# Two transformer blocks in float32: how the experts are dealt to the two sides of the array, and in which order their weights are loaded

## The chip, the cores and the metric

One core of a Trainium2 chip runs the whole program. The metric is device microseconds of one execution.

## The reference

All data are float32. A first block (attention, a window attention, pooling, a long convolution, then a mixture of experts) is followed by a second block (a recurrence with attention, retention, two SwiGLU layers). The change lies in the mixture of experts of the first block, on 512 tokens of width 1024:

```python
N_EXPERTS, TOP_K, D_MODEL, D_EXPERT = 16, 2, 1024, 512
# each token picks one group of four experts, then the best two of that group
gates = jnp.sum(jax.nn.one_hot(eidx, N_EXPERTS) * w[..., None], axis=1)
for e in range(N_EXPERTS):
    h = jax.nn.silu(x @ w1[e]) * (x @ w3[e])
    out = out + gates[:, e:e + 1] * (h @ w2[e])
```

The inputs that the reference draws (seed 0) send this many of the 1,024 (token, expert) pairs to experts 0 to 15: 34, 40, 52, 30, 54, 16, 66, 66, 47, 127, 193, 87, 52, 44, 63, 53. In units of 64 tokens, rounded up, these are 1, 1, 1, 1, 1, 1, 2, 2, 1, 2, 4, 2, 1, 1, 1, 1, together 23.

## The kernel before, in words

TensorE (PE) multiplies, VectorE (DVE) and ScalarE (ACT) take its products, GpSimd (POOL) gathers and scatters token rows, and SP issues the loads of weights. All weights come as tiles of 512 KB into `weights_and_work`.

**A job.** The expert stage is a loop of `n_jobs` jobs on PE (`experts()`). One job works on two units at once: 64 tokens of an expert on side 0 of the array (b = 0) and 64 tokens of another on side 1 (b = 1). Each side has one buffer of 12 tiles (`expert_w[b]`) for its expert: tiles 0 to 3 and 4 to 7 hold w1 and w3, tiles 8 to 11 hold w2. I call these three groups of four tiles phases 0, 1 and 2. A job runs phases 0 and 1 (L1353, 64 matmuls), turns the token rows of the next job (L1337) and the hidden rows of this one (L1362), and runs phase 2 (L1371, 32 matmuls). Behind each tile it raises `e_passed`. At its head it reads one number, `landing`, into a register (L1344), and ahead of each tile it waits once, for that tile's semaphore `e_landed[s]` to reach it.

**The deal.** Even experts go to side 0 and odd ones to side 1, in order of their number, each for as many jobs as it has units. `n_jobs` is the larger of the two sums. `first` is the job with which an expert begins.

**The loads.** SP loads experts 0 and 1 ahead of the stage. The other 14 are loaded in order of `first`, in a loop with a turn for each expert (L804). A turn reads three numbers (L805 to L807), and for each of the 12 tiles a fourth (L809), waits until that tile of that buffer has been passed by the job before and until the semaphore's last load has landed, and issues the DMA (L812). So the second of two experts that begin with the same job is issued behind all 12 tiles of the first.

**The tables.** The numbers that SP and PE read are made by DVE on tiny tiles in `router()`: it ranks the tokens (`rank`), places them in jobs, and makes `gather_i`, then `landing_i`, `n_jobs_i` (`jobs_ready`), `result_i`, and last `order_i`, `after_i` and `buffer_i` (`order_set`). `link` makes DVE wait for its own last instruction. PE's `experts()` begins with a wait for `jobs_ready`, and POOL gathers the rows of the first job as soon as `gather_i` is set.

Of the kernel before, what the change touches and what calls it, by code (L numbers as in the profile page):

```python
# [6 lines left out]
ALU = mybir.AluOpType  # L7
ACT = mybir.ActivationFunctionType
AX_X = mybir.AxisListType.X
# [8 lines left out]
S = 512  # L18
# [41 lines left out]
EXPERT_TILES = 12  # L60
UNIT = 64
# [123 lines left out]
def plan():  # L185
# [62 lines left out]
    r["ms_meta"], = b.many(1)  # L248
# [122 lines left out]
def two_blocks(nc, d):  # L371
# [5 lines left out]
    with ExitStack() as ctx:  # L377
# [69 lines left out]
        buffer_of = tiny[:, 460:460 + EXPERTS]  # L447
# [81 lines left out]
        order_hot, order_t = piece(arena, 14000, EXPERTS, EXPERTS), piece(arena, 14260, EXPERTS, EXPERTS)  # L529
        order, first, landing_e = (arena[:, a:a + EXPERTS] for a in (15640, 15656, 15672))  # L530
        order_f = piece(arena, 15700, 3, EXPERTS)
        order_i, landed_i, buffer_i = (arena[:, 15760 + EXPERTS * i:15760 + EXPERTS * (i + 1)].bitcast(I32) for i in range(3))
        after_f = piece(arena, 15940, EXPERT_TILES, EXPERTS)
        after_i = piece(arena, 16140, EXPERT_TILES, EXPERTS).bitcast(I32)
        over = piece(arena, 17700, JOBS, EXPERTS)
        landing_f = arena[:, 15820:15820 + JOBS]
        landing_i = arena[:, 15880:15880 + JOBS].bitcast(I32)
# [96 lines left out]
        e_landed = [sem(f"expert_tile_in_{i}") for i in range(RING)]  # L634
        e_passed, order_set = sem("expert_tiles_passed"), sem("expert_order_set")
# [88 lines left out]
        def _(sp):  # L724
# [53 lines left out]
            def first_of(e, i):  # L778
                if e:
                    sp.wait_ge(e_landed[slots[i]], 16)  # L780
                elif i < RING - 4:
                    sem_, value = read_by(before + i - RING)
                    sp.wait_ge(sem_, value)
                else:
                    ready(sp, r["w_out"][2 * (i - RING + 4) + 1])
                sp.dma_start(expert_w[e][:, slots[i], :], d["experts"][e, i]).then_inc(e_landed[slots[i]], 16)

            for i in range(RING - 4):
                first_of(0, i)
            ready(sp, r["OT", ST - 1][1])  # L790
            for i in range(RING - 4):
                first_of(1, i)
            for e in range(2):
                for i in range(RING - 4, RING):
                    first_of(e, i)
# [124 lines left out]
        def _(pe):  # L920
# [405 lines left out]

            def experts():
# [15 lines left out]
                with pe.Fori(0, n_jobs) as it:  # L1343
                    landing = pe.value_load(landing_i[0:1, bass.ds(it, 1)], min_val=16, max_val=16 * EXPERTS)  # L1344
# [810 lines left out]
        def _(dve):  # L2155
# [292 lines left out]
            def router():  # L2448
# [896 lines left out]
```

## Time and profile before

| | |
|---|---|
| median of 3 runs | 2518.15 us (2515.71 to 2518.84) |
| profiled execution, its own time | 2521.37 us |
| its span in the profile | 2519.5 us |
| mean granted clock of TensorE | 0.963 |
| PE busy | 2358.8 us, 94% of the span |
| expert stage, first matmul of the first job to the end of the last job | 579.86 to 914.70 us |

Times in the views are microseconds from the start of the span; a trailing q on an engine (PEldq, SPq) is its sequencer, which waits, branches, reads registers and issues DMAs while the engine itself may still work. PEclk is the granted share of the full TensorE clock.

### The profile page before, as it was taken

The page shows a single profiled execution, that of the slowest core. Times are in us where ns is not written, and L with a number is a line of the kernel's source. Part 1 is how long each engine was busy: PE and PEld are TensorE (multiplying, and loading weights), DVE is VectorE, ACT ScalarE, POOL GpSimd, SP SyncE. Part 2 cuts the span into 40 slices and gives each one's busy share as a digit, 9 for nine tenths or more (in the row PEclk, how much of TensorE's full clock was granted, in tenths as well). Part 3 has the DMA queues.
Part 4 walks back from the last instruction along what each step waited for, and adds up shares of the span by engine and source line. Part 5 has one row for each costly group of instructions (what it writes and reads, how often), then busy time and mean ns, then how long its engine had stood idle before and what let it go on. Part 6 is the DMA issues. An engine that isn't in the chain of part 4 may idle for free.

```text
span 2519.5 us, 28945 instructions
## 1 busy us (share of the span) xinstructions
PE 2358.8 (94%) x10176; PEld 1657.1 (66%) x10177; DVE 970.0 (39%) x1756; ACT 522.3 (21%) x1097; POOL 133.3 (5%) x150
## 2 busy tenths in 40 slices
PE   6999999977689889899999999899999999999999
PEld 2564456643234348668888888476675778888888
DVE  7331267552000032553434433334333354335521
ACT  2300046531111133442111100111212202111100
POOL 1000044400001010000000000000000000000000
PEclk9999999887899999989999999899999999999999
DMA  9301124256977972112222222131121122322220
GB/s 337 130 10 51 33 74 186 107 210 238 386 264 269 329 300 64 38 34 68 84 84 87 87 68 100 68 101 58 41 96 56 56 67 86 92 90 84 84 103 31
DMA packets 81185, 299.24 MB, mean 119 GB/s; under 512 B 9024, under 2 KB 9024, under 8 KB 80464
## 3 DMA queue, kind: packets, MB, share of 16 engines
q1 hardware_dynamic: 75312, 272.14, 31.1%
q0 software_dynamic: 5792, 26.00, 2.8%
q8 instruction: 54, 0.88, 0.1%
q14 instruction: 27, 0.22, 0.0%
HBM read 283.94 MB, written 14.16 MB: 118 GB/s over the span
## 4 chain that ended last, share of the span: by engine, by line
PE 86%; DVE 6%; ACT 3%; issue 2%; DMA 2%; SPq 2%; DVEq 0%; POOL 0%; ACTq 0%; POOLq 0%
PE products L1523 39%; PE products L954 7%; PE products L1353 7%; PE products L1133 6%; PE products L1428 3%; PE products L1371 3%; PE products L1670 2%; PE products L1184 2%; PE products L1605 2%; PE products L1040 1%; PE products L1262 1%; PE products L1478 1%; PE products L1087 1%; PE products L1097 1%; PE products L1197 1%
## 5 line engine op out<-in xcount | busy, mean ns | idle before, releaser
L1523 PE MATMUL products<-normed,weights_and_work 128*128 128x264 f32 (+1 forms) x1520 | 347.7, 384 | 0.0
L1523 PEld LDWEIGHTS products<-normed,weights_and_work 128*128 128x128 f32 x1520 | 288.5, 190 | 49.2 <-issue 3.4
L1766 ACT ACTIVATE weights_and_work<-products 128x256 f32<-128x256 f32 (+4 forms) x243 | 108.9, 466 | 602.7 <-PE products L1523 156.4
L1353 PE MATMUL products<-weights_and_work 128*64 128x512 f32 x768 | 180.7, 631 | 48.7 <-DMA weights_and_work<-in_experts 48.0
L1523 PE MATMUL products<-weights_and_work,mixed 128*128 128x256 f32 (+1 forms) x800 | 182.3, 382 | 0.8 <-ACT weights_and_work L1766 0.8
L1353 PEld LDWEIGHTS products<-weights_and_work 128*64 128x64 f32 x768 | 65.4, 146 | 162.3 <-issue 160.7
L1523 PEld LDWEIGHTS products<-weights_and_work,mixed 128*128 128x128 f32 x800 | 151.8, 190 | 24.4 <-ACT weights_and_work L1766 1.6
L1133 PE MATMUL products<-weights_and_work,normed 128*128 128x512 f32 x352 | 154.8, 601 | 8.4 <-DVE normed L2176 8.4
L1523 PE MATMUL products<-weights_and_work 128*128 128x256 f32 (+1 forms) x672 | 151.0, 385 | 8.2 <-DVE residual L3061 5.2
L1523 PE MATMUL products<-weights_and_work,normed 128*128 128x264 f32 (+1 forms) x704 | 155.6, 382 | 0.0
L1523 PE MATMUL products<-normed,mixed 128*128 128x264 f32 (+1 forms) x672 | 154.1, 382 | 0.0
L1523 PEld LDWEIGHTS products<-weights_and_work 128*128 128x128 f32 x672 | 128.8, 192 | 29.4 <-issue 7.0
L1523 PEld LDWEIGHTS products<-weights_and_work,normed 128*128 128x128 f32 x704 | 133.8, 190 | 20.5
L1523 PEld LDWEIGHTS products<-normed,mixed 128*128 128x128 f32 x672 | 127.7, 190 | 19.6
L1133 PEld LDWEIGHTS products<-weights_and_work,normed 128*128 128x128 f32 x352 | 67.9, 193 | 94.2 <-issue 94.2
L2618 DVE TENSOR_TENSOR weights_and_work<-products,weights_and_work 128x256 f32<-128x256 f32 x24 | 9.1, 419 | 300.3 <-PE products L1353 300.3
L954 PE MATMUL products<-normed,weights_and_work 128*128 128x512 f32 (+1 forms) x320 | 124.2, 549 | 0.0
L954 PEld LDWEIGHTS products<-normed,weights_and_work 128*128 128x128 f32 x320 | 60.8, 190 | 63.3 <-issue 61.2
L2907 DVE TENSOR_TENSOR residual<-products,residual 128x264 f32<-128x264 f32 (+1 forms) x56 | 23.9, 427 | 189.8 <-PE products L1523 181.2
L1523 PE MATMUL products<-mixed,weights_and_work 128*128 128x264 f32 x384 | 91.7, 387 | 1.1 <-ACT weights_and_work L1766 1.1
L1371 PE MATMUL products<-weights_and_work 128*64 128x512 f32 x384 | 85.0, 594 | 4.7 <-DVE weights_and_work L2621 4.7
L1523 PEld LDWEIGHTS products<-mixed,weights_and_work 128*128 128x128 f32 x384 | 72.6, 190 | 15.0 <-ACT weights_and_work L1766 2.8
(518 smaller groups left out, 2912.6 us busy)
## 6 DMA issues: line engine op xcount, KB each, us to landing
weights_and_work<-in_weights SPq DMA_DIRECT2D x303, 512.0 KB, 4.3
weights_and_work<-in_experts SPq DMA_DIRECT2D x192, 512.0 KB, 5.5
results<-normed SPq DMA_DIRECT2D x8, 512.0 KB, 6.9
residual<-in_x POOLq DMA_DIRECT2D x1, 2048.0 KB, 16.5
weights_and_work<-in_dft_half POOLq DMA_DIRECT2D x1, 2048.0 KB, 8.5
token_rows<-mixed SPq DMA_DIRECT2D x4, 512.0 KB, 3.1
normed<-results SPq DMA_DIRECT2D x4, 512.0 KB, 6.8
mixed<-results SPq DMA_DIRECT2D x4, 512.0 KB, 7.4
```

Of the source, the lines that this page charges most:

```text
L954: m = pe.matmul(bank(p, n), w[:, k, :], acts[:, k, at:at + n], start=(k == 0), stop=(k == kt - 1))
L1040: m = pe.matmul(bank(p), w[:, c, tt, :], filt[:, tt, :, 0, :] if c == 0 else diff[:, tt], start=(tt == 0), stop=(tt == ST - 1))
L1087: m = pe.matmul(ps[:, p.bank, c * 256:(c + 1) * 256], dft[:, c, tt, kt * P:(kt + 1) * P], sig_t[:, tt], start=(tt == 0), stop=(tt == ST - 1))
L1133: m = pe.matmul(ps[0:n_tok, p.bank, :], acts(k), w[k // 2][:, k % 2, :], start=(k == 0), stop=(k == KT - 1))
L1184: m = pe.matmul(ps[:, p.bank, 0:DH], prob_t[:, a, kt, :], vals[:, kt, a, h * DH:(h + 1) * DH], start=(kt == 0), stop=(kt == NKT - 1))
L1353: m = pe.matmul(ps[UNIT * b:UNIT * (b + 1), side, :], job_t[:, k, UNIT * b:UNIT * (b + 1)], expert_w[b][:, s, at:at + 512], start=(k == 0) ...
L1371: m = pe.matmul(ps[UNIT * b:UNIT * (b + 1), 4 + half, :], hid_t[:, k, UNIT * b:UNIT * (b + 1)], expert_w[b][:, s, half * 512:(half + 1) * ...
L1428: m = pe.matmul(both_halves(p)[:, j], w[:, k, :], h2[:, k, at:at + n], start=(k == 0), stop=(k == KT - 1))
L1523: m = pe.matmul(bank(p, n), left(k), right(k), start=(fresh and k == 0), stop=(k == kt - 1), skip_group_check=True)
L1605: m = pe.matmul(bank(p, width), w[4][:, k] if k < 8 else w[5][:, k - 5], t4[:, k, 0:width], start=False, stop=(k == H - 1), skip_group_che ...
L1670: m = pe.matmul(ps[:, p.bank, at:S], ret_v[0:n, t, i * P:(i + 1) * P], ret_s[0:n, t, at:S], start=(t == 0), stop=(t == 4), skip_group_chec ...
L1766: act.activation(out, src, ACT.Copy, scale=scale).then_inc(bank_free[p.bank], 1)
```

## The change

The experts are ranked by units, the largest first, with expert 0 forced to the front and expert 1 to the back. Going down the ranks, experts are given to side 0 until half of all units are gone; the others go to side 1, which is run from the back of the ranks. So with the units above side 0 gets experts 0, 10, 6, 7, 9 (1 + 4 + 2 + 2 + 2 = 11 units) and side 1 gets 1, 15, 14, 13, 12, 8, 5, 4, 3, 2, 11 (12 units).

The load of an expert is cut into its three phases, 48 parts in all, numbered by job, then phase, then side. Part n uses lane set n modulo 3, four semaphores each (one for each tile of a part). SP's loop takes three parts a turn. It reads one number for the turn, two for each part and one for each tile. PE reads nine numbers at the head of a job, one for each phase and lane set, and waits for three semaphores ahead of each tile. DVE's tables are made anew, with one entry on each partition; PE turns them into rows by two sets of small matmuls (9 and 6) that stand behind `ms_meta` and ahead of `experts()`.

```diff
 
 EXPERT_TILES = 12
+PHASES, PHASE_TILES = 3, 4
+LOADS = 16 * PHASES
+LANES = 3
...
-    r["ms_meta"], = b.many(1)
+    r["ms_meta"], r["landings"], r["loads"] = b.many(3)
...
+            by_phase = d["experts"].rearrange("e (g i) p t -> (e g) i p t", g=PHASES)
+
+            def first_of(n):
+                phase, e = n // 2, n % 2
+                for i in range(PHASE_TILES):
+                    s = slots[PHASE_TILES * phase + i]
+                    lane_in = e_landed[n % LANES * PHASE_TILES + i]
+                    if n >= LANES:
+                        sp.wait_ge(lane_in, 16 * (n // LANES))
+                    if e == 0 and phase < 2:
+                        sem_, value = read_by(before + PHASE_TILES * phase + i - RING)
+                        sp.wait_ge(sem_, value)
+                    elif e == 0:
+                        ready(sp, r["w_out"][2 * i + 1])
+                    sp.dma_start(expert_w[e][:, s, :], by_phase[PHASES * e + phase, i]).then_inc(lane_in, 16)
+
+            first_of(0)
             ready(sp, r["OT", ST - 1][1])
+            for n in range(1, 2 * PHASES):
+                first_of(n)
...
-            with sp.Fori(2, EXPERTS) as it:
-                e = sp.value_load(order_i[0:1, bass.ds(it, 1)], min_val=0, max_val=EXPERTS - 1)
-                landed_by = sp.value_load(landed_i[0:1, bass.ds(it, 1)], min_val=0, max_val=16 * EXPERTS)
-                to = sp.value_load(buffer_i[0:1, bass.ds(it, 1)], min_val=0, max_val=RING * TILE)
-                for i, s in enumerate(slots):
-                    passed_by = sp.value_load(after_i[0:1, i, bass.ds(it, 1)], min_val=1, max_val=MAX_JOBS * EXPERT_TILES)
-                    sp.wait_ge(e_passed, passed_by)
-                    sp.wait_ge(e_landed[s], landed_by)
-                    sp.dma_start(weights_and_work[:, bass.ds(to + s * TILE, TILE)], d["experts"][e, i]).then_inc(e_landed[s], 16)
+            with sp.Fori(2 * PHASES // LANES, LOADS // LANES) as it:
+                landed_by = sp.value_load(landed_i[0:1, bass.ds(it, 1)], min_val=0, max_val=16 * LOADS)
+                for n in range(LANES):
+                    at = bass.ds(it * LANES + n, 1)
+                    part = sp.value_load(loads_i[0:1, 0, at], min_val=0, max_val=LOADS - 1)
+                    to = sp.value_load(loads_i[0:1, 1, at], min_val=0, max_val=(2 * RING - PHASE_TILES) * TILE)
+                    for i in range(PHASE_TILES):
+                        lane_in = e_landed[n * PHASE_TILES + i]
+                        passed_by = sp.value_load(loads_i[0:1, 2 + i, at], min_val=1, max_val=MAX_JOBS * EXPERT_TILES)
+                        sp.wait_ge(e_passed, passed_by)
+                        sp.wait_ge(lane_in, landed_by)
+                        sp.dma_start(weights_and_work[:, bass.ds(to + i * TILE, TILE)], by_phase[part, i]).then_inc(lane_in, 16)
...
+                for n, (p, columns, count) in enumerate(((r["landings"], landing_col, LANES * PHASES), (r["loads"], load_col, 6))):
+                    fill(p)
+                    pe.wait_ge(columns_set, n + 1)
+                    for v in range(count):
+                        m = pe.matmul(ps[0:1, p.bank, 48 * v:48 * (v + 1)], columns[:, v:v + 1], ident[:, 0:48], start=True, stop=True)
+                    finish(p, m)
...
-                    landing = pe.value_load(landing_i[0:1, bass.ds(it, 1)], min_val=16, max_val=16 * EXPERTS)
+                    landing = [[pe.value_load(landing_i[0:1, PHASES * n + phase, bass.ds(it, 1)], min_val=16, max_val=16 * LOADS)
+                                for n in range(LANES)] for phase in range(PHASES)]
+
+                    def tile_in(phase, i):
+                        for n in range(LANES):
+                            pe.wait_ge(e_landed[n * PHASE_TILES + i], landing[phase][n])
+
...
-                            pe.wait_ge(e_landed[s], landing)
+                            tile_in(side, pair)
...
-                        pe.wait_ge(e_landed[s], landing)
+                        tile_in(2, k)
...
-                HALF = EXPERTS // 2
-                for b in range(2):
-                    of = slice(b * HALF, (b + 1) * HALF)
-                    ins = dve.tensor_tensor_scan(end[:, of], ones[:, 0:HALF], units[:, of], b * UNIT / 2.0, ALU.mult, ALU.add)
-                link(ins)
-                link(tt_(key, end, units, ALU.subtract))
+                dve.tensor_reduce(total, units, AX_X, ALU.add)
+                link(tt_(key, units, size_bias, ALU.add))
+                link(tt_(sooner_t, bcast(key, 1, EXPERTS), bcast(key, 2, EXPERTS), ALU.is_gt))
+                link(tt_(sooner_t, sooner_t, bcast(units, 1, EXPERTS), ALU.mult))
+                link(dve.tensor_reduce(begun_before, sooner_t, AX_X, ALU.add))
+                link(stt(past, begun_before, 2.0, units, ALU.mult, ALU.add))
+                link(ts(past, past, total, None, ALU.subtract))
+                ts(side, past, 0.0, None, ALU.is_ge)
+                link(ts(past, past, 0.0, None, ALU.max))
+                link(tt_(begun_before, begun_before, past, ALU.subtract))
+                link(stt(key, side, UNIT / 2.0, begun_before, ALU.mult, ALU.add))
                 link(ts(tmp, rank, -(UNIT - 1) / 2.0, ROUND_UNIT, ALU.add, ALU.add))
                 link(stt(rank, tmp, ROUND_UNIT, rank, ALU.subtract, ALU.add))
-                for t in range(ST):
-                    ins = stt(rank[:, t].rearrange("p (h b) -> p h b", b=2), key.rearrange("p (b h) -> p h b", b=2), 2.0,
-                              rank[:, t].rearrange("p (h b) -> p h b", b=2), ALU.mult, ALU.add)
-                link(ins)
+                link(stt(rank, bcast(key, 1, ST), 2.0, rank, ALU.mult, ALU.add))
...
+                link(ts(first, begun_before, 1.0 / UNIT, None, ALU.mult))
+                link(tt_(sooner_t, bcast(first, 1, EXPERTS), bcast(first, 2, EXPERTS), ALU.is_lt))
+                link(dve.tensor_reduce(sooner, sooner_t, AX_X, ALU.add))
+                link(tt_(same_t, bcast(first, 1, EXPERTS), bcast(first, 2, EXPERTS), ALU.is_equal))
+                link(dve.tensor_reduce(same, same_t, AX_X, ALU.add))
+                link(stt(within, same, -1.0, side, ALU.add, ALU.mult))
+                link(stt(load_base, sooner, float(PHASES), within, ALU.mult, ALU.add))
+                for phase in range(PHASES):
+                    ins = stt(load_no[:, phase], same, float(phase), load_base, ALU.mult, ALU.add)
+                link(ins)
+                link(ts(begun_e, first, partition, None, ALU.is_le))
+                link(tt_(load_t, load_no, bcast(begun_e, 1, PHASES), ALU.mult))
+                link(dve.tensor_reduce(last_load, load_t, AX_X, ALU.max))
+                for n in range(LANES):
+                    ins = ts(landing_col[:, PHASES * n:PHASES * (n + 1)], last_load, float(LANES - 1 - n), 1.0 / LANES, ALU.add, ALU.mult)
+                link(ins)
+                link(ts(landing_col, landing_col, ROUND, None, ALU.add))
+                link(ts(landing_col, landing_col, ROUND, None, ALU.subtract))
+                ts(landing_col, landing_col, 1.0, 16.0, ALU.max, ALU.mult).then_inc(columns_set, 1)
+                dve.wait_ge(columns_set, 1)
+
+                for phase in range(PHASES):
+                    ts(load_ids[:, phase], lane[:, 0:EXPERTS], float(PHASES), float(phase), ALU.mult, ALU.add)
+                    ts(after_e[:, phase], first, float(EXPERT_TILES), float(PHASE_TILES * phase + 1 - EXPERT_TILES), ALU.mult, ALU.add)
+                    ts(buffer_e[:, phase], side, float(RING * TILE),
+                       float((START["ab_qk"] + PHASE_TILES * phase) % RING * TILE), ALU.mult, ALU.add)
+                link(ts(load_hot, load_no, partition, None, ALU.is_equal))
+                for v, of in enumerate((load_ids, buffer_e, after_e)):
+                    link(tt_(load_t, load_hot, of, ALU.mult))
+                    link(dve.tensor_reduce(load_col[:, v:v + 1], load_t.rearrange("p g e -> p (g e)"), AX_X, ALU.add))
+                ts(landed_i_f, lane[:, 0:LOADS], 16.0, None, ALU.mult)
+                ts(load_col[:, 3:6], lane[:, 1:4], load_col[:, 2:3], None, ALU.add).then_inc(columns_set, 1)
+                dve.wait_ge(columns_set, 2)
+
+                p = r["landings"]
+                ready(dve, p)
+                link(tt_(end, begun_before, units, ALU.add))
+                link(dve.tensor_reduce(last_f, end, AX_X, ALU.max))
                 link(ts(count[:, 0:1], last_f, 1.0 / UNIT, None, ALU.mult))
                 link(ts(last_f, count[:, 0:1], 1.0, None, ALU.subtract))
-                dve.tensor_copy(landing_i, landing_f)
+                dve.tensor_copy(landing_i[0:1].rearrange("p g j -> p (g j)"), ps[0:1, p.bank, 0:48 * LANES * PHASES]).then_inc(bank_free[p.bank], 1)
...
+                p = r["loads"]
+                ready(dve, p)
+                dve.tensor_copy(loads_i[0:1].rearrange("p g j -> p (g j)"), ps[0:1, p.bank, 0:48 * 6]).then_inc(bank_free[p.bank], 1)
+                read(dve, p)
+                dve.tensor_copy(landed_i, landed_i_f).then_inc(order_set, 1)
```

## Rows read from the trace of the kernel before

**Rows 1.** The page: busy time by engine; DMA issues (KB each, us to landing).

```profile
PE 2358.8 (94%) x10176; PEld 1657.1 (66%) x10177; DVE 970.0 (39%) x1756; ACT 522.3 (21%) x1097; POOL 133.3 (5%) x150
...
weights_and_work<-in_experts SPq DMA_DIRECT2D x192, 512.0 KB, 5.5
```

**Rows 2.** Timeline of PE, expert stage: start us, us, instructions, idle before.

```profile
579.86 16.69 PE L1353 MATMUL products<-weights_and_work 128*64 128x512 f32 x64 [0.69 <-ACT weights_and_work L1930]
...
598.40 7.09 PE L1371 MATMUL products<-weights_and_work 128*64 128x512 f32 x32 [0.39 <-DVE weights_and_work L2621]
613.78 16.79 PE L1353 MATMUL products<-weights_and_work 128*64 128x512 f32 x64 [8.29 <-DMA weights_and_work<-in_experts]
...
650.91 15.30 PE L1353 MATMUL products<-weights_and_work 128*64 128x512 f32 x64 [11.40 <-DMA weights_and_work<-in_experts]
...
686.98 16.04 PE L1353 MATMUL products<-weights_and_work 128*64 128x512 f32 x64 [11.83 <-DMA weights_and_work<-in_experts]
...
742.74 15.47 PE L1353 MATMUL products<-weights_and_work 128*64 128x512 f32 x64 [8.11 <-DMA weights_and_work<-in_experts]
...
789.62 13.93 PE L1353 MATMUL products<-weights_and_work 128*64 128x512 f32 x64
...
805.40 7.09 PE L1371 MATMUL products<-weights_and_work 128*64 128x512 f32 x32 [0.39 <-DVE weights_and_work L2621]
812.29 13.93 PE L1353 MATMUL products<-weights_and_work 128*64 128x512 f32 x64
...
866.22 16.86 PE L1353 MATMUL products<-weights_and_work 128*64 128x512 f32 x64 [8.39 <-DMA weights_and_work<-in_experts]
...
907.61 7.09 PE L1371 MATMUL products<-weights_and_work 128*64 128x512 f32 x32 [0.39 <-DVE weights_and_work L2621]
```

**Rows 3.** The matmuls of L1353 in the whole trace.

```profile
L1353 PE MATMUL products<-weights_and_work x768: 592/592/1116, 579.9 to 905.2; 128*64 128x512 f32 x192
```

**Rows 4.** SP sequencer, by lines: two windows around changes of expert, one run.

```profile
L812 SPq DMA_DIRECT2D weights_and_work<-in_experts x2: 342/344/346, 623.9 to 627.4; - x2
...
L806 SPq TENSOR_LOAD <-weights_and_work x1: 273/273/273, 625.3 to 625.3; - x1
...
L807 SPq TENSOR_LOAD <-weights_and_work x1: 263/263/263, 626.0 to 626.0; - x1
...
L812 SPq DMA_DIRECT2D weights_and_work<-in_experts x11: 342/342/345, 628.7 to 641.4; - x11
```

**Rows 5.** PE sequencer between two jobs without a wait (window 798 to 815).

```profile
L1343 PEldq ALU_OP  x1: 32/32/32, 808.0 to 808.0; - x1
...
L1344 PEldq TENSOR_LOAD <-weights_and_work x1: 312/312/312, 808.5 to 808.5; - x1
...
L1349 PEldq EVENT_SEMAPHORE  x1: 51/51/51, 809.3 to 809.3; - x1
```

**Rows 6.** Timeline of DVE ahead of the first job.

```profile
571.86 0.18 DVE L2568 TENSOR_SCALAR weights_and_work<-weights_and_work 128x8 f32<-128x8 f32 x1
572.07 0.17 DVE L2569 TENSOR_SCALAR weights_and_work<-weights_and_work 128x8 f32<-128x8 f32 x1
572.28 0.42 DVE L2570 TENSOR_TENSOR weights_and_work<-weights_and_work 128x256 f32<-128x256 f32 x1
572.74 0.42 DVE L2571 TENSOR_REDUCE weights_and_work<-weights_and_work 128x16 f32<-128x256 f32 x1
...
576.06 0.14 DVE L2581 CAST weights_and_work<-weights_and_work 128x1 int32<-128x1 f32 x1
```

**Rows 7.** Timeline of PE: first turning of rows, and a short idle elsewhere.

```profile
139.29 0.89 PE L1087 MATMUL products<-weights_and_work 128*128 128x256 f32 x3 [2.48 <-ACT weights_and_work L1766]
...
577.21 1.97 PE L1337 MATMUL products<-const_sb,normed 128*128 128x128 f32 x8 [6.06 <-DMA normed<-token_rows,weights_and_work]
```

**Rows 8.** Windows: us, busy us by engine, PEclk, DMA share, GB/s.

```profile
136.00:172.00 36.00, 31.20 (x120) 21.07 (x119) 14.63 (x25) 3.00 (x9) 0.00 (x0) 1.00 0.00 0
...
675.00:687.00 12.00, 0.17 (x4) 0.05 (x2) 0.00 (x0) 2.55 (x3) 1.38 (x3) 0.61 1.02 414
```

More of the change, by code:

```diff
@@ L446, in two_blocks @@
         unused_row = tiny[:, 425:426]
-        buffer_of = tiny[:, 460:460 + EXPERTS]
+        side = tiny[:, 460:460 + EXPERTS]
         sub_ms, sub_ln, sub_rs = (tiny[:, a:a + HEADS] for a in (428, 432, 436))
@@ L528, in two_blocks @@
         result_f, slot_t = arena[:, 13760:13760 + JOBS], arena[:, 13790:13790 + JOBS]
[L529 to L537, printed above, removed]
+        same_t, sooner_t = piece(arena, 14000, EXPERTS, EXPERTS), piece(arena, 14260, EXPERTS, EXPERTS)
+        sooner, first, same, within, load_base = (arena[:, a:a + EXPERTS] for a in range(15640, 15720, EXPERTS))
+        load_no, landing_e = piece(arena, 15720, PHASES, EXPERTS), piece(arena, 15768, PHASES, EXPERTS)
+        begun_e, load_t, load_hot = arena[:, 15816:15832], piece(arena, 15832, PHASES, EXPERTS), piece(arena, 15880, PHASES, EXPERTS)
+        after_e, buffer_e = piece(arena, 15928, PHASES, EXPERTS), piece(arena, 15976, PHASES, EXPERTS)
+        load_col, last_load = arena[:, 16024:16030], arena[:, 16030:16033]
+        landing_col = arena[:, 14540:14540 + LANES * PHASES]
+        landed_i_f = arena[:, 16292:16292 + LOADS]
+        size_bias, total = arena[:, 16340:16340 + EXPERTS], arena[:, 16356:16357]
+        begun_before, past = arena[:, 16360:16360 + EXPERTS], arena[:, 14520:14520 + EXPERTS]
+        load_ids = piece(arena, 16040, PHASES, EXPERTS)
+        landing_i = piece(arena, 19040, LANES * PHASES, 48).bitcast(I32)
+        loads_i = piece(arena, 17644, 6, 48).bitcast(I32)
+        landed_i = arena[:, 18028:18028 + LOADS].bitcast(I32)
         gather_f = arena[:, 18470:18470 + JOBS]
@@ L633, in two_blocks @@
             "token_rows_stored", "places_ready", "gather_indices_set", "result_indices_set"))
-        e_landed = [sem(f"expert_tile_in_{i}") for i in range(RING)]
-        e_passed, order_set = sem("expert_tiles_passed"), sem("expert_order_set")
+        e_landed = [sem(f"expert_tile_in_{i}") for i in range(LANES * PHASE_TILES)]
+        e_passed, order_set, columns_set = sem("expert_tiles_passed"), sem("expert_loads_set"), sem("table_columns_set")
         rows_turned, hid_turned, hid_taken = sem("job_rows_transposed"), sem("hidden_transposed"), sem("hidden_taken")
@@ L2454, in router @@
                 tt_(gain_ab, par("final_g"), par("norm_ab"), ALU.mult)
[L2455 to L2456 removed]
+                link(ts(size_bias, lane[:, 0:EXPERTS], -1.0, None, ALU.mult))
+                dve.memset(size_bias[:, 0:1], float(4 * S))
+                dve.memset(size_bias[:, 1:2], -float(4 * S))
                 dve.memset(picked[:, ST], 0.0)
@@ L2567, in router @@
                 read(dve, p)
-                link(ts(first[:, 0:HALF], key[:, 0:HALF], 1.0 / UNIT, None, ALU.mult))
-                link(ts(first[:, HALF:EXPERTS], key[:, HALF:EXPERTS], -UNIT / 2.0, 1.0 / UNIT, ALU.add, ALU.mult))
-                link(tt_(order_t, bcast(key, 1, EXPERTS), bcast(key, 2, EXPERTS), ALU.is_lt))
-                link(dve.tensor_reduce(order, order_t, AX_X, ALU.add))
-                link(ts(landing_e, order, 16.0, 16.0, ALU.mult, ALU.add))
-                link(tt_(over, bcast(first, 1, JOBS), bcast(lane[:, 0:JOBS], 2, EXPERTS), ALU.is_le))
@@ L2574, in router @@
-                link(tt_(over, over, bcast(landing_e, 1, JOBS), ALU.mult))
-                link(dve.tensor_reduce(landing_f, over, AX_X, ALU.max))
-                link(ts(last_f, end[:, EXPERTS - 1:EXPERTS], -UNIT / 2.0, end[:, HALF - 1:HALF], ALU.add, ALU.max))
+                link(ts(first, begun_before, 1.0 / UNIT, None, ALU.mult))
+                link(tt_(sooner_t, bcast(first, 1, EXPERTS), bcast(first, 2, EXPERTS), ALU.is_lt))
+                link(dve.tensor_reduce(sooner, sooner_t, AX_X, ALU.add))
```

36 lines of the change are left out of this document (1 added, 35 removed).

## The prediction

> **What bounds the kernel now.** The page comes first: PE is busy for 94% of the span [rows 1], so only what holds PE up, or gives it less to do, moves the time. The change touches the expert stage alone, so next I read PE's timeline there [rows 2]. The 768 matmuls of L1353 at 64 a job are 12 jobs [rows 3]. A job that waits for nothing lasts 812.29 - 789.62 = 22.67 us. The stage runs from 579.86 to 907.61 + 7.09 = 914.70, that is 334.8 us, of which 12 jobs need 272.0. The first job's L1353 lasts 16.69 instead of 13.93 us, which is 2.8 more. What is left, 60.0 us, hangs on five waits for expert weights: idle times of 8.29, 11.40, 11.83, 8.11 and 8.39 us (48.0 together), and behind each an L1353 of 15.30 to 16.86 instead of 13.93 us (10.8 together); 1.2 us are small change at the same five places.
>
> The reader should see where these five stand. By the units of the inputs the even experts begin with jobs 0, 1, 2, 3, 5, 6, 10, 11 and the odd ones with 0, 1, 2, 3, 5, 7, 9, 10. Two experts begin together with jobs 1, 2, 3, 5 and 10, and the timeline idles ahead of exactly these. Jobs 6, 7, 9 and 11, with one new expert each, start on time. The second expert of a pair is issued behind the twelfth tile of the first, which the job before passes at its very end; 3.5 us from issue to issue across a change of expert [rows 4] and a landing of some 5 us [rows 1] make the 8.1 to 8.4 us.
>
> **The number of jobs.** It stays 12: 23 units on two sides need 12 jobs however they are dealt. The new deal has sides of 11 and 12 units. Experts then begin on side 0 with jobs 0, 1, 5, 7, 9 and on side 1 with 0 to 10. Pairs are left at jobs 1, 5, 7, 9. Matmuls, rows gathered and bytes loaded do not change.
>
> **What the order of parts removes.** In a pair, each phase is now loaded for both sides before the next phase. The second expert no longer waits for the end of the job. All 60.0 us of stalls and slow restarts go at first: -60. What takes their place is worked out below.
>
> **SP's pace.** In a run SP issues a tile each (641.4 - 628.7) / 10 = 1.27 us [rows 4]. Successive reads of a register start 0.65 us apart (625.3, 626.0, and the two ends round a little; [rows 4]). An expert takes 11 x 1.27 + 3.5 = 17.5 us of SP today. Three reads a turn become seven, so it will take 17.5 + 4 x 0.65 = 20.1 us; between 19.5, if the branch costs less, and 21.5, if the index of three parts a turn needs more register work.
>
> A lone pair needs 40.2 us from the first tile passed, 1.7 us into the job before, and a landing of 5: its last tile is there 47 us after that job began. PE wants that tile at 26.0 (below) + 21 = 47 us. So the pairs of jobs 1 and 5 are just covered: nothing. But from job 5 on there are three experts in each two jobs: 60.3 us of SP against 2 x 26.0 = 52 of PE. The first such two jobs have slack ahead of them (one expert a job before); the pairs of jobs 7 and 9 each come 8.4 us late. That is +17, and since PE then idles within a job and restarts at the lower clock, some 2 us more each by the slow L1353 of today: +4.
>
> The Trainium skill (DMA: Bandwidth & Descriptors, Issuing engines are not separate DMA queues) says that all transfers share 16 DMA engines and that the issuer's time is usually small beside the transfer. By it three lane sets add no bandwidth, and the engines, not SP, would set the pace; that is the rival C below. The rows leave both open, since the engines are full too in a run (share 1.02 at 414 GB/s, [rows 8]).
>
> **PE's head of a job.** Today the sequencer ends a job's loop at 808.0, reads its one register in a 0.312 us operation at 808.5, and comes to the first tile's wait at 809.3 [rows 5]; the first matmul can go at 812.29 [rows 2]. So it has a lead of 2.9 us. Eight more reads, at SP's 0.65 apart, are 5.2 us. Also, two of the three waits per tile are new instructions of 0.051 us [rows 5] with their decoding, about 0.1 us; ten of them lie between the start of L1371 and the first tile of the next job, where the lead is made: 0.9. The rest of the lead covers 2.8. A job then grows by 5.2 + 0.9 - 2.8 = 3.3 us (2.2 if the waits cost nothing, 4.4 if they cost 0.2 each), to 26.0. Eleven of these: +36. They are behind nothing else in jobs without a DMA wait; the register reads of a job with a late first tile would be hidden, but none of the four pairs has its first tile late.
>
> **Ahead of the first job.** A small linked DVE operation takes 0.21 us from start to start, one of 256 elements 0.46 [rows 6]. Before the places of the tokens there are three wide and six narrow linked ones, and two loose ones, more, and two scans, a subtraction and three narrow operations fewer: +2.0 us. Then L2568 to L2581, 571.86 to 576.20, hold `jobs_ready`: 4.3 us. The new chain to the first set of columns has 4 wide, 9 narrow and 6 loose operations, 4.4 us; to the second 9 loose and 8 narrow ones, 2.9; to `jobs_ready` four narrow ones, a copy of 432 elements and two casts, 1.5. Together 8.8, that is +4.5. PE's nine and six tiny matmuls fit behind this chain: at the 0.25 us each of the eight turnings at 577.21 [rows 7] they take 2.2 and 1.5 us. PE then has the eight more reads, 5.2 us. Today its first matmul comes 2.65 us after the turning began (577.21 to 579.86), and its own head needs some 1.1 of these; the other 1.6 cover a part of the reads. The gather of the rows, which ended the wait at 577.21 [rows 7], comes 2 us later and is covered. Sum: 2.0 + 4.5 + 5.2 - 1.6 = +10, between 8 and 12. SP's first load waits for the first tile passed, so its later tables cost nothing (they are ready some 3 us before that). The loads of experts 0 and 1 only change their order and are over long before the stage.
>
> **The sum.** -60 + 17 + 4 + 36 + 10 = +7 us. Each microsecond more at the head of a job moves this by 11 - 4 = 7 (two late pairs get 2 us more cover each). The profiled execution lasted 2521.37 us; its sum would be 2528. It lies 3.2 above the median of 2518.15, so I predict 2525.
>
> **Rivals.**
>
> B, faster: the sequencer hides the reads. If PE's lead covers the whole head, a job stays at 22.67 us; the late pairs are then 60.3 - 45.3 = 15 us each. -60 + 30 + 4 + 10 = -16: 2502. For it: part of the lead is measured to hide one read now. Against: the lead is 2.9 us and the reads 5.2. It turns the sign below a head of some 2.3 us, and it is measurably faster below 1.6. Chance 0.12.
>
> C: DMA engines set the pace instead of SP. 512 KB at 414 GB/s are 1.27 us, so an expert takes 15.2 us and three of them 45.7, less than two jobs: no late pair. +7 - 21 = -14: 2504. Against: today's loop already stands still for 3.5 us at a change of expert while the engines could go on. Chance 0.10.
>
> D, much slower: PE drops to its lower clock at every head. An idle of 2.48 us at 139.29 [rows 7] left the granted clock at 1.00 [rows 8]; idles of 8.1 us and more cost 1.4 to 2.9 us each. A head leaves PE idle for some 3.3 us, between the two. Nine heads without another stall at 2.2 us: +20, in all +27: 2545. The Trainium skill (TensorE: Matmul & The Clock Gate, HAM oscillation) describes a kernel whose short waits, one for each tile, bring a cold restart every time; by it D is what happens once a head is long enough. Chance 0.15.
>
> My forecast, costs and gain nearly equal with a small loss, gets 0.55 and its own range -2 to +16; mixtures of the above get 0.08.
>
> **Range and chances.** 5 us, 0.2%, is about what a measurement of this kernel can tell from no change. The forecast's own range is 2516 to 2534. To leave out no more than two in ten it has to reach B and C below, and the bounds of the head and of SP's pace above (+8 and +8): 2502 to 2542. Faster by over 0.2%: B, C and a little of the mixtures, 0.25. Within: the lower part of the forecast, 0.27. Slower: its upper part and D, 0.48.
>
> **What would show it.** In the changed kernel's profile: L1353 x768 still; no idle ahead of L1353 put down to in_experts with the 8 to 12 us of today; idles of about 3.3 us put down to issue ahead of most jobs; nine register reads on PE's sequencer at each head; the first L1353 near 590; DMA waits inside jobs 7 and 9 only, with SP issuing an expert in about 20 us. The prediction is wrong if the heads are under 2 us, if SP's waits for PE remain in jobs 5 to 10 (then it is not the bound), or if PEclk falls at heads.

## The result, and the profile after

The changed kernel takes 2542.73 us (median of 4 runs, 2540.3 to 2544.87) against 2518.49 us of the kernel before (4 runs). The ratio is 1.0097, 95% interval 1.0079 to 1.0114: 24 us slower. I had predicted 2525 with a range of 2502 to 2542, and rival D had said 2545.

The timeline of PE in the expert stage of the changed kernel; L1379 is what L1353 was, L1397 what L1371 was:

```profile
583.85 1.97 PE L1357 MATMUL products<-const_sb,normed 128*128 128x128 f32 x8 [2.62 <-issue]
591.34 15.46 PE L1379 MATMUL products<-weights_and_work 128*64 128x512 f32 x64 [5.52 <-issue]
...
618.82 15.38 PE L1379 MATMUL products<-weights_and_work 128*64 128x512 f32 x64 [3.08 <-issue]
...
646.76 16.76 PE L1379 MATMUL products<-weights_and_work 128*64 128x512 f32 x64 [3.63 <-issue]
...
675.56 15.65 PE L1379 MATMUL products<-weights_and_work 128*64 128x512 f32 x64 [3.11 <-DMA weights_and_work<-in_experts]
...
703.21 15.65 PE L1379 MATMUL products<-weights_and_work 128*64 128x512 f32 x64 [3.06 <-issue]
...
730.86 15.65 PE L1379 MATMUL products<-weights_and_work 128*64 128x512 f32 x64 [3.06 <-issue]
...
758.96 15.28 PE L1379 MATMUL products<-weights_and_work 128*64 128x512 f32 x64 [3.52 <-issue]
...
786.21 8.44 PE L1379 MATMUL products<-weights_and_work 128*64 128x512 f32 x32 [3.03 <-issue]
796.05 7.09 PE L1379 MATMUL products<-weights_and_work 128*64 128x512 f32 x32 [1.40 <-DMA weights_and_work<-in_experts]
...
809.14 8.78 PE L1397 MATMUL products<-weights_and_work 128*64 128x512 f32 x32 [4.54 <-DMA weights_and_work<-in_experts]
821.86 15.65 PE L1379 MATMUL products<-weights_and_work 128*64 128x512 f32 x64 [3.94 <-DMA weights_and_work<-in_experts]
...
849.50 8.78 PE L1379 MATMUL products<-weights_and_work 128*64 128x512 f32 x32 [3.05 <-DMA weights_and_work<-in_experts]
858.60 7.09 PE L1379 MATMUL products<-weights_and_work 128*64 128x512 f32 x32 [0.32 <-DMA weights_and_work<-in_experts]
...
870.88 5.34 PE L1397 MATMUL products<-weights_and_work 128*64 128x512 f32 x16 [3.73 <-DMA weights_and_work<-in_experts]
876.66 3.65 PE L1397 MATMUL products<-weights_and_work 128*64 128x512 f32 x16 [0.44 <-DMA weights_and_work<-in_experts]
...
886.31 16.45 PE L1379 MATMUL products<-weights_and_work 128*64 128x512 f32 x64 [6.00 <-issue]
...
914.75 15.65 PE L1379 MATMUL products<-weights_and_work 128*64 128x512 f32 x64 [3.05 <-issue]
...
932.26 7.09 PE L1397 MATMUL products<-weights_and_work 128*64 128x512 f32 x32 [0.39 <-DVE weights_and_work L2668]
```

Set this beside [rows 2]. The idles of 8 to 12 us are gone. In their place an idle of some 3.1 us stands ahead of every job, most put down to issue, and behind it L1379 lasts 15.65 us, not 13.93. An undisturbed job, from 703.21 to 730.86, lasts 27.65 us; before it was 22.67. Inside jobs 7 and 9 there are waits for weights; with what follows them they make these jobs 35.65 and 36.81 us long, counted to the first matmul of the next job.

Windows of the same trace, one undisturbed job and then job 7 (us; busy us of PE, PEld, DVE, ACT and POOL; PEclk, DMA share, GB/s):

```profile
703.00:730.80 27.80, 24.20 (x108) 9.88 (x108) 1.51 (x4) 4.23 (x6) 3.24 (x9) 0.94 0.78 277
...
786.00:821.80 35.80, 25.77 (x108) 9.39 (x108) 1.51 (x4) 4.23 (x6) 3.73 (x9) 0.91 0.97 346
```

The same view of the kernel before, over a job that waits for nothing:

```profile
789.60:812.00 22.40, 22.01 (x110) 9.42 (x108) 1.51 (x4) 4.23 (x6) 3.09 (x8) 1.00 0.34 131
```

The granted clock is 0.94 over a job that waits for no data; before it was 1.00. The lower of the two levels comes back at each head.

The sequencers, by lines: PE's reads at one head (L1364) and in all, its waits ahead of the first job (L1349), and SP's issues over one turn of its loop (L825):

```profile
L1364 PEldq TENSOR_LOAD <-weights_and_work x9: 296/300/320, 639.7 to 645.8; - x9
```

```profile
L1364 PEldq TENSOR_LOAD <-weights_and_work x108: 295/300/1303, 584.1 to 913.8; - x108
```

```profile
L1349 PEldq EVENT_SEMAPHORE  x3: 51/51/2412, 580.2 to 582.7; - x3
```

```profile
L825 SPq DMA_DIRECT2D weights_and_work<-in_experts x13: 342/343/395, 749.6 to 771.1; - x13
```

Nine reads start between 639.7 and 645.8, 0.76 us apart (0.75 is usual). SP issues 12 tiles from 749.6 to 771.1, 21.4 us; over the last six turns, by the starts of their first issues, the mean is 20.7.

### The profile page after: what moved, and what is told of

It is laid out like the page before. It is cut to its first block, busy times and chain, and to the rows that moved or that the text cites. A ratio compares the mean times of both kernels' runs of the same rounds, so it can differ in the third digit from the quotient of the medians.

```text
span 2542.2 us, 29787 instructions
## 1 busy us (share of the span) xinstructions
PE 2373.7 (93%) x10206; PEld 1661.3 (65%) x10207; DVE 971.6 (38%) x1780; ACT 522.8 (21%) x1097; POOL 133.6 (5%) x150
## 4 chain that ended last, share of the span: by engine, by line
PE 82%; DVE 6%; issue 4%; SPq 4%; ACT 3%; DMA 2%; DVEq 0%; POOL 0%; ACTq 0%; POOLq 0%
PE products L1549 39%; PE products L967 7%; PE products L1146 6%; PE products L1379 5%; PE products L1454 3%; PE products L1197 2%; PE products L1696 2%; DMA weights_and_work<-in_experts 2%; PE products L1631 2%; PE products L1397 1%; PE products L1053 1%; SPq L822 1%; SPq L825 1%; PE products L1275 1%; PE products L1504 1%
## 5 line engine op out<-in xcount | busy, mean ns | idle before, releaser
L1379 PE MATMUL products<-weights_and_work 128*64 128x512 f32 x768 | 189.0, 654 | 45.8 <-issue 34.0
L1379 PEld LDWEIGHTS products<-weights_and_work 128*64 128x64 f32 x768 | 66.7, 150 | 167.5 <-issue 158.5
L1397 PE MATMUL products<-weights_and_work 128*64 128x512 f32 x384 | 88.6, 614 | 12.6 <-DMA weights_and_work<-in_experts 8.7
```

What stands on the lines that cost most here:

```text
L1379: m = pe.matmul(ps[UNIT * b:UNIT * (b + 1), side, :], job_t[:, k, UNIT * b:UNIT * (b + 1)], expert_w[b][:, s, at:at + 512], start=(k == 0) ...
L1397: m = pe.matmul(ps[UNIT * b:UNIT * (b + 1), 4 + half, :], hid_t[:, k, UNIT * b:UNIT * (b + 1)], expert_w[b][:, s, half * 512:(half + 1) * ...
```

## The experiments

**Fewer reads at PE's head.** Three kernels move a few of the nine reads from the head of the job to the phase that needs them; all waits stay.

```diff
-                    landing = [[pe.value_load(landing_i[0:1, PHASES * n + phase, bass.ds(it, 1)], min_val=16, max_val=16 * LOADS)
-                                for n in range(LANES)] for phase in range(PHASES)]
...
+                    landing = [[read_landing(phase, n) for n in range(EARLY[phase])] for phase in range(PHASES)]
+
+                    def read_rest(phase):
+                        landing[phase] += [read_landing(phase, n) for n in range(EARLY[phase], LANES)]
...
                     for side in range(2):
+                        read_rest(side)
...
+                    read_rest(2)
                     pe.wait_ge(job_read, it * 16 + 32)
```

`read_landing` is the read that stood there. EARLY, the reads at the head by phase, is [3, 3, 2] with eight (e2), [3, 3, 1] with seven (e10) and [3, 3, 0] with six (e3).

> The changed kernel with only one of the nine reads moved (the last, to ahead of phase 2). Reads are 0.75 us apart, so the idle at a head should shrink from 3.06 to about 2.3 us. If the granted clock falls because of this idle and 2.3 us are too short for that (an idle of 2.48 us kept it in the kernel before), the head costs 2.3 us without the slow restart: 11 x (0.75 + 1.7) = 27 us less, about 2516 with late pairs a little later (+5): 2520. If the clock falls anyway, 11 x 0.75 less: about 2536.

> The changed kernel with three of the nine reads moved (those of phase 2, ahead of the turning of rows). Idle at a head 3.06 - 2.25 = 0.8 us and no slow restart: 11 x (2.25 + 1.7) = 43 less, late pairs later by 2 x 8: about 2514. Without any effect of the clock: 11 x 2.25 less, late pairs +9: about 2526.

> Seven of PE's nine reads at the head of a job, between e3 (six: idle 0.8 us, no slow restart) and e2 (eight: idle 2.3 us, a slow restart each time). Idle about 1.55 us. If the slow restart belongs to any idle above one microsecond it is there (L1379 15.65 us, total near 2535); if it needs more, L1379 stays near 13.95 us and the total is 2523 to 2528.

Measured, one run each: 2541.8 with eight, 2525.9 with seven, 2523.2 us with six. Heads of jobs that have no other wait, in the timelines of PE with eight, seven and six reads:

```profile
704.24 15.65 PE L1387 MATMUL products<-weights_and_work 128*64 128x512 f32 x64 [2.32 <-issue]
...
731.15 15.65 PE L1387 MATMUL products<-weights_and_work 128*64 128x512 f32 x64 [2.32 <-issue]
```

```profile
669.46 13.95 PE L1387 MATMUL products<-weights_and_work 128*64 128x512 f32 x64 [1.53 <-issue]
...
718.36 13.95 PE L1387 MATMUL products<-weights_and_work 128*64 128x512 f32 x64 [1.56 <-issue]
```

```profile
690.45 13.95 PE L1387 MATMUL products<-weights_and_work 128*64 128x512 f32 x64 [0.81 <-issue]
```

Each read taken away shortens the idle by 0.75 us: 3.06, 2.32, 1.55, 0.8. That is the lead of 2.9 us against one read less each time, with nothing left for the extra waits. From eight to seven the slow restart goes as a whole: L1387 lasts 13.95 us, and a job without another wait lasts 24.45 us (669.46 to 718.36 is two of them) instead of 26.91, which is 0.75 less for the read and 1.70 for the clock. My guess for eight reads was wrong: an idle of 2.3 us does bring the lower clock here.

The totals do not show this step cleanly. They fall by 16 us from eight to seven, but 9 of these lie ahead of the expert stage, where the two kernels have the same code: the matmuls of L1332 start at 573.21 us with eight and at 563.92 with seven, and no run shows why. The stage alone lasts 348.0 us with nine reads, 341.5 with eight, 335.2 with seven and 333.3 with six. Eleven jobs shorter by 2.46 us would have given 27 from eight to seven; only 6 came, because shorter jobs make the weights come late, as below.

**Nine reads in the kernel before.** The same cost put into the other kernel (e4):

```diff
-                    landing = pe.value_load(landing_i[0:1, bass.ds(it, 1)], min_val=16, max_val=16 * EXPERTS)
+                    for _ in range(9):
+                        landing = pe.value_load(landing_i[0:1, bass.ds(it, 1)], min_val=16, max_val=16 * EXPERTS)
```

> The kernel before with nine reads of the one number at the head of each job instead of one; nothing else. Six heads there have no DMA wait (jobs 4, 6, 7, 8, 9, 11). The theory (idle of 3.1 and a slow restart of 1.7 us each): 6 x 4.9 = 29, and some 4 ahead of the first job: +33, about 2551; the five heads with a DMA wait hide the reads. Without the clock: 6 x 3.1 + 4 = +23, 2541. If reads were not what costs at the head: 2518.

Measured 2540.85 us, ratio 1.0084 (1.0056 to 1.0112). The heads without a DMA wait, in PE's timeline:

```profile
712.91 15.65 PE L1354 MATMUL products<-weights_and_work 128*64 128x512 f32 x64 [2.10 <-issue]
...
773.82 13.96 PE L1354 MATMUL products<-weights_and_work 128*64 128x512 f32 x64 [2.08 <-issue]
...
798.78 15.65 PE L1354 MATMUL products<-weights_and_work 128*64 128x512 f32 x64 [2.07 <-issue]
...
825.43 15.65 PE L1354 MATMUL products<-weights_and_work 128*64 128x512 f32 x64 [2.06 <-issue]
...
852.06 13.95 PE L1354 MATMUL products<-weights_and_work 128*64 128x512 f32 x64 [2.05 <-issue]
...
910.90 15.65 PE L1354 MATMUL products<-weights_and_work 128*64 128x512 f32 x64 [2.09 <-issue]
```

Eight more reads of a number make the kernel before nearly as slow as the whole change does. Its idles are 2.05 to 2.10 us, and four of six restarts are slow: this is the edge. The six heads cost 12.4 us of idle and 4 x 1.7 = 6.9 of clock, and the idle ahead of the first job grew from 0.69 to 4.34 us; together 23, and 22 were measured.

I had expected the idle of 3.1 us that nine reads leave in the changed kernel. The sequencers show why it is a microsecond less; first PE's reads at a head of this kernel, then what stands beside the nine reads at a head of the changed one:

```profile
L1345 PEldq TENSOR_LOAD <-weights_and_work x9: 296/301/307, 792.7 to 797.9; - x9
L1345 PEldq FUSED_REGOPS  x9: 146/146/156, 793.1 to 798.3; - x9
```

```profile
L1364 PEldq FUSED_REGOPS  x17: 46/151/151, 640.1 to 646.2; - x17
```

Here the reads start 0.65 us apart, as SP's do. In the changed kernel each read but the first has a second register operation (17 for 9 reads), and they start 0.75 to 0.76 apart. Eight times this difference of 0.1 is most of the microsecond. Both kernels leave nearly the same lead, 3.1 us here (8 x 0.65 - 2.07) and 2.9 to 3.0 there, although the changed one has three waits for each tile.

**All reads at their phase (e1).** EARLY is [3, 0, 0]; three reads are left at the head.

> The changed kernel with PE's nine reads split: three at the head of a job, three ahead of phase 1 and three ahead of phase 2. All waits stay. The theory (each head of a job idles PE for 3.1 us because nine reads outlast the sequencer's lead, and each such idle brings 1.7 us of matmuls at the lower clock): heads without idle, L1379 at 13.9 us instead of 15.65, a job of 22.7 us instead of 27.65, and since SP stays as it is the late pairs of jobs 7 and 9 grow from 8 to about 17 us each: 11 x 5.0 - 18 = 37 us less than the changed kernel, and 4 us less ahead of the first job: about 2502. Rival 1 (the three waits for each tile, not the reads, hold PE up): the heads stay as they are, 2540. Rival 2 (the reads only move the idle to the phases): the head's idle shrinks by 4.5 us but 2 us appear ahead of phase 1 and of phase 2, 2525 to 2540.

Measured 2518.01 us, ratio to the kernel before 0.9998 (0.9982 to 1.0013). 25 us are back, not 41. The timeline of PE, jobs 2 and 3 and then the pair of job 7:

```profile
636.02 13.95 PE L1387 MATMUL products<-weights_and_work 128*64 128x512 f32 x64 [0.47 <-issue]
...
658.72 13.93 PE L1387 MATMUL products<-weights_and_work 128*64 128x512 f32 x64
...
767.75 8.45 PE L1387 MATMUL products<-weights_and_work 128*64 128x512 f32 x32 [4.17 <-DMA weights_and_work<-in_experts]
780.37 8.78 PE L1387 MATMUL products<-weights_and_work 128*64 128x512 f32 x32 [4.17 <-DMA weights_and_work<-in_experts]
...
793.35 8.78 PE L1406 MATMUL products<-weights_and_work 128*64 128x512 f32 x32 [2.73 <-DMA weights_and_work<-in_experts]
```

The head is free: 22.7 us from 636.02 to 658.72, L1387 at 13.95. But a shorter job gives SP less time. With jobs of 22.7 us the pairs of jobs 1 and 5 come late too. The stage lasts 911.07 - 582.49 = 328.6 us, and 12 jobs of 22.67 are 272.0. Of the 56.5 us between them 1.9 are the first job's matmuls at the lower clock, and some 55 are late parts and what follows them.

**SP's reads.** One read for a part instead of four, alone (e6) and together with the reads of PE at their phase (e5):

```diff
+                    passed_by = sp.value_load(loads_i[0:1, 2, at], min_val=1, max_val=MAX_JOBS * EXPERT_TILES)
                     for i in range(PHASE_TILES):
                         lane_in = e_landed[n * PHASE_TILES + i]
-                        passed_by = sp.value_load(loads_i[0:1, 2 + i, at], min_val=1, max_val=MAX_JOBS * EXPERT_TILES)
-                        sp.wait_ge(e_passed, passed_by)
+                        sp.wait_ge(e_passed, passed_by + i)
```

> The changed kernel with SP's one read for each part alone; PE's heads keep their nine reads. The late pairs of jobs 7 and 9 (8.0 and 9.2 us) go, the heads stay at 3.1 us of idle and 1.7 us of slow restart: about 2525. If the late pairs were not SP's doing: 2542.

> The changed kernel with PE's nine reads split over the phases (as in e1_reads_at_phase) and with one read for each part in SP's loop in place of four (the tile's number is added in the wait). If e1 was held at 2518 by SP, which still needs 20.7 us for an expert, it is now the DMA engines' 1.28 us a tile, 15.4 us an expert, three of them 46 against two jobs of 45.3: no late pair, jobs of 22.7 us, the stage 276 us instead of 329: 2518 - 52 = about 2466. Rival (something else, the waits for tiles or the landing, holds PE in e1's pairs): 2500 or more.

Measured 2519.1 us alone (one run) and 2473.79 together with the reads at their phase, ratio 0.9841 (0.9819 to 0.9863). Alone it takes out the waits within jobs 7 and 9 and leaves the heads. The stage lasts 327.6 us instead of 348.0, 20 less, of which the late pairs were 17; the other 4 of the 24 us lie ahead of it, in code that this edit leaves alone. PE's timeline of jobs 7 to 9:

```profile
781.65 15.34 PE L1379 MATMUL products<-weights_and_work 128*64 128x512 f32 x64 [3.04 <-DMA weights_and_work<-in_experts]
...
809.00 15.32 PE L1379 MATMUL products<-weights_and_work 128*64 128x512 f32 x64 [3.07 <-issue]
...
836.32 15.31 PE L1379 MATMUL products<-weights_and_work 128*64 128x512 f32 x64 [3.07 <-DMA weights_and_work<-in_experts]
```

Together both costs go. PE's timeline of the pairs of jobs 5 and 7:

```profile
695.67 13.93 PE L1387 MATMUL products<-weights_and_work 128*64 128x512 f32 x64
...
712.11 7.09 PE L1406 MATMUL products<-weights_and_work 128*64 128x512 f32 x32 [1.05 <-DMA weights_and_work<-in_experts]
...
741.67 7.07 PE L1387 MATMUL products<-weights_and_work 128*64 128x512 f32 x32
752.69 9.58 PE L1387 MATMUL products<-weights_and_work 128*64 128x512 f32 x32 [3.95 <-DMA weights_and_work<-in_experts]
...
771.01 13.93 PE L1387 MATMUL products<-weights_and_work 128*64 128x512 f32 x64
```

The stage lasts 286.5 us, against 273.8 for 12 jobs with the first one's slow matmuls. What is left are waits for weights with the DMA engines full; the windows of jobs 6 and 7:

```profile
719.00:741.70 22.70, 22.31 (x111) 9.50 (x110) 1.51 (x4) 4.23 (x6) 3.08 (x8) 1.00 1.03 411
741.70:771.00 29.30, 24.96 (x110) 9.40 (x108) 1.51 (x4) 4.23 (x6) 3.09 (x8) 0.88 1.03 411
```

In job 7 of the changed kernel they moved 346 GB/s. I had expected 2466 with no late pair, and the total is 8 us above that. This version still beats both kernels.

**The deal and the order of loads, one without the other.** The first kernel (e7) puts the new ranking of experts, with the lines that go with it, into the kernel before. The other two (e8, e9) put the even and odd deal into the changed kernel and into the one with both kinds of reads cut; this is their edit.

```diff
-                dve.tensor_reduce(total, units, AX_X, ALU.add)
-                link(tt_(key, units, size_bias, ALU.add))
...
-                link(tt_(begun_before, begun_before, past, ALU.subtract))
+                of_side = "p (h b) -> p h b"
+                dve.memset(side.rearrange(of_side, b=2)[:, :, 0], 0.0)
+                dve.memset(side.rearrange(of_side, b=2)[:, :, 1], 1.0)
+                for b in range(2):
+                    ins = dve.tensor_tensor_scan(past.rearrange(of_side, b=2)[:, :, b], ones[:, 0:EXPERTS // 2],
+                                                 units.rearrange(of_side, b=2)[:, :, b], 0.0, ALU.mult, ALU.add)
+                link(ins)
+                link(tt_(begun_before, past, units, ALU.subtract))
```

> The kernel before with the new deal alone: experts ranked and dealt as in the change, weights loaded expert by expert as before, one read at PE's head, one wait a tile. Pairs stand at jobs 1, 5, 7 and 9 instead of 1, 2, 3, 5 and 10, each with an idle of about 8.3 us and a slow restart of 2.5: 43 instead of 60 us, and 2 us more of tables ahead of the first job: about 2503. If the deal brings nothing by itself: 2518.

> The changed kernel with the deal of before (even and odd experts in their order); parts, lanes, reads and waits as in the change. Pairs at jobs 1, 2, 3 need 41 us of SP each against jobs of 27.6: two of them come 14 us late, the pair of job 5 follows them at once and has one job of slack, that of job 10 is lone: about 28 to 35 us of late pairs instead of 17: 2552 to 2560. If the deal makes no difference: 2542.

> e5_both (reads split over the phases, one read for each part on SP) with the deal of before. What the ranking of experts is worth once PE and SP are free: pairs at jobs 1, 2, 3 bring two experts of 15.4 us against jobs of 22.7, so that the pairs of jobs 2 and 3 come 8 us late each, against some 12 us of lateness in all with the new deal; three narrow DVE operations fewer ahead. About 2478 to 2484 against 2474. If the deal matters more (as it did with slow loads, 11 us): 2485 or more. If it does not matter: 2474.

Measured 2498.39 us for e7, ratio 0.9925 (0.9909 to 0.9942); 2553.3 for e8 (one run); 2486.34 for e9, ratio 0.9874 (0.9857 to 0.9890). So the ranking alone gains 18 us against the kernel before. Its pairs explain 13 of them: in the traces the stage is 14.6 us shorter (320.2 against 334.8), and the ranking costs 2.0 us ahead of it. The rest lies in code that the edit leaves alone and is not explained: the matmuls ahead of the ranks start at 550.04 us in the trace of e7 (L1311) and at 558.52 in that of the kernel before (L1307). In the changed kernel the ranking hid 11 us of the loss (2553.3 against 2542.7, one run). In e9 PE waits in jobs 2 and 3, as expected, and the ranking is worth some 12 us there, more than the 4 to 10 that I had expected; 9.7 of them lie in the stage (296.2 against 286.5).

**SP's pace in the kernel before (e11).**

```diff
+                passed_by = sp.value_load(after_i[0:1, 0, bass.ds(it, 1)], min_val=1, max_val=MAX_JOBS * EXPERT_TILES)
                 for i, s in enumerate(slots):
-                    passed_by = sp.value_load(after_i[0:1, i, bass.ds(it, 1)], min_val=1, max_val=MAX_JOBS * EXPERT_TILES)
-                    sp.wait_ge(e_passed, passed_by)
+                    sp.wait_ge(e_passed, passed_by + i)
```

> The kernel before with one read for each expert in SP's loop in place of twelve for its tiles (the tile's number is added in the wait). If SP's pace was part of the price of pairs there: the change of expert still costs its 2.3 us of reads, but an expert that follows at once is issued in 10 us instead of 15 and lands at 15.4; the idles of 11.4 and 11.8 us at jobs 2 and 3 shrink to 8 or 9 and the others stay at 8.3: about 2511. If only the order matters (second expert behind the last tile of the first): 2517.

Measured 2515.59 us, ratio 0.9996 (0.9986 to 1.0007): no difference that can be told. The idles of jobs 2 and 3 fell to 8.90 and 9.24 us, as expected, but those of jobs 1 and 5 rose to 9.92 and 8.80. All five sum to 45.3 us instead of 48.0. So what the pairs cost there was the order; SP's pace was at most 3 us of it.

## Why the prediction was wrong

The step that failed is the one that left the clock out of PE's head, the choice between the forecast and rival D. I gave D 0.15. The nearest row was one idle of 2.48 us elsewhere, behind which the clock stayed [rows 7, 8], and I let it stand for eleven idles of 3.3. The term was missing from the sum: 11 x 1.72 = 19 us. The runs showed in its place that the clock falls at every head: L1379 lasts 15.65 instead of 13.93 us behind an idle of 3.06, and at 1.55 us of idle (e10) this stops. The Trainium skill (TensorE: Matmul & The Clock Gate, HAM oscillation), which I had set beside D, describes such a cold restart behind every short wait; the trace after agrees, with 15.65 for 13.93 us.

Adding 19 to the forecast gives 2544, and 2542.7 was measured, but that this fits so well is in part luck. By the prediction's own rule a longer job gives the late pairs more time, so that 1.72 us a head are worth about 12 and not 19 us, and the total would be 2537. What makes up the rest are terms that it had too small or not at all, below.

The other steps, one by one:

- The five stalls went: right, -60. The number of jobs stayed 12: right.
- SP's pace: 20.1 us for an expert forecast, 20.7 measured. The late pairs: 17 + 4 forecast, 8.0 and 9.2 us measured, and made up in another way. Waits for weights are only 5.6 us in job 7 (1.40 and 4.54, less the 0.39 that L1397 waits in every job) and 4.1 in job 9 (0.32, 3.73 and 0.44, less 0.39), since jobs of 27.65 us gave SP more time. Each of the two jobs has a second slow restart inside, 1.7 and 1.9 us in L1397, as forecast. The rest was not foreseen: where L1397 waits for a tile, the sequencer comes to its next nine reads with less lead. They start 3.1 and 2.0 us ahead of the end of L1397 (814.8 and 878.3) instead of 4.0 (696.2, in an undisturbed job), which costs 0.9 and 1.9 us at the heads of jobs 8 and 10, and one read of job 10 took 1.303 us instead of 0.300. Some 2.7 us more lie in jobs 1, 2, 5 and 10.
- PE's head: right in the sum, 3.3 us, and wrong in its parts, which is luck. A plain read does cost PE the 0.65 us of SP (e4), but these need a register operation more, so they cost 0.75 and eight of them 6.0. The extra waits, forecast at 0.9, cost nothing that shows (e2, e3, e4, e10). They were also fewer than I had counted: PE's sequencer has 156 EVENT_SEMAPHORE at L1369 where it had 12 at L1349, one more for each tile and not two.
- Ahead of the first job: +10 forecast. From the copy of the ranks (559.79 after, 561.12 before) to the first matmul it is 31.6 us after and 18.7 before, +12.8. The two DVE chains took +2.1 and +4.5 as forecast; the reads left 4.8, not 3.6; and 1.3 us come from a wait that I had not seen. PE's `experts()` waits for all banks, also that of the second table, until DVE has copied it: the 2.412 us EVENT_SEMAPHORE of L1349 above.
- Rival B (reads hidden) is out by e2, e3, e4 and e10. Rival C (DMA engines set the pace) is out by e6 and e5: with fewer reads on SP the late pairs of 17 us go.

The prediction's own sign of being wrong, that PEclk falls at heads, was met. The sum by the measured terms, for the stage: 272.0 for 12 jobs, 1.5 for the first one's cold matmuls, 11 x (3.26 + 1.72) = 54.8 for heads (3.26 is what an undisturbed job grew by without the clock, 27.65 - 22.67 - 1.72), 17.2 for late pairs, 2.7 in small change, together 348.2; the trace has 939.35 - 591.34 = 348.0. Before it had 334.8.

My expectation for e1 missed another coupling: I counted two late pairs where shorter jobs made four.

## What to carry to other kernels

Finer bookkeeping in a loop with registers is paid by the sequencer: count the reads at the head of a turn, compare them with its lead over the engine, and read a number only just ahead of its use. An idle of TensorE that comes back at every turn can cost half as much again in the restart (1.7 us behind 3.1 here), so price it with that and, where the trace has only one such idle, with both answers. Single runs of two kernels can differ by 9 us in code that they share, so compare the stage that was changed and not the totals alone. A cure for a wait (here -60 us) is judged only after its own reads, tables and waits have been priced: the ranking alone gained 18 us, the whole change lost 24, and the change with six of PE's nine reads moved and nine of SP's nineteen for 12 tiles taken away gained 43.

## What the runs showed of the hardware

In this loop idles of 0.8 to 1.6 us between jobs left the next L1387 at 13.95 us; at 2.05 to 2.10 us four of six were followed by a 15.65 us one (e4); with 2.3 us (e2) and 3.1 us (after) at every head each one was. But an idle's length alone does not tell. A single one of 2.48 us in another stage had left the clock up, and so did one of 3.00 us inside job 9 of e5, where PE had worked at the full clock since job 8 began:

```profile
803.75 7.09 PE L1387 MATMUL products<-weights_and_work 128*64 128x512 f32 x32 [3.00 <-DMA weights_and_work<-in_experts]
```

A register read of PE took 0.300 us as an operation; from one to the next it took 0.65 us where it was plain (e4) and 0.75 with one more register operation of 0.046 us (after). SP's took 0.65. An extra wait on a semaphore long reached took the sequencer 0.051 us and did not show in PE's time.
